# Another order of block products, the last units behind the last group, and joins and additions on GpSimd

## The reference

```
hm = rms_norm(x, g_pre_mlp[i])
f = jnp.square(jax.nn.relu(hm @ w_mlp_up[i])) @ w_mlp_down[i]
x = x + rms_norm(f, g_post_mlp[i])

gate = jax.nn.sigmoid(rms_norm(x, g_pre_ple[i]) @ w_ple_gate[i])
e = p[i] @ w_ple_proj[i]
x = x + rms_norm(gate * e, g_post_ple[i])
```

## Time and profile before

| | us |
|---|---|
| median of 3 runs | 2764.78 |
| the profiled execution | 2765.39 |
| its span | 2763.6 |
| TensorE busy | 2697.1 (98%) |
| VectorE busy | 2041.0 (74%) |
| ScalarE busy | 1395.6 (50%) |
| GpSimd busy | 291.1 (11%) |
| waits of TensorE's L1093 for DVE L2441, L2489 | 16.1 and 7.4 |

### The profile page before, as it was taken

One profiled execution on the slowest core, in us unless ns is written; L12 is line 12 of the kernel. 1 busy time (PEld: TensorE's weight loads), 2 busy tenths in 40 slices (PEclk: granted clock), 3 DMA queues, 4 the chain that ended last, 5 costly groups with the idle time before them and its releaser, 6 DMA issues.

```text
span 2763.6 us, 34607 instructions
## 1 busy us (share of the span) xinstructions
PE 2697.1 (98%) x12816; PEld 2242.8 (81%) x12816; DVE 2041.0 (74%) x2767; ACT 1395.6 (50%) x2399; POOL 291.1 (11%) x329
## 2 busy tenths in 40 slices
PE   8999999999999999989999999999999999999897
PEld 7878888888888888867888788888888888888685
DVE  5468888385777777788866688883767777777886
ACT  5337888464333333346644478884633333333473
POOL 0320000001111111100013200000010111111000
PEclk9999999999999999999999999999999999999998
DMA  4211112431111111132332111143311111112332
GB/s 163 78 57 48 33 34 95 157 111 65 62 54 54 54 39 57 58 136 85 106 113 76 51 40 34 29 146 120 137 39 48 60 62 51 51 38 67 123 106 76
DMA packets 86519, 208.28 MB, mean 75 GB/s; under 512 B 9040, under 2 KB 37840, under 8 KB 85328
## 3 DMA queue, kind: packets, MB, share of 16 engines
q1 hardware_dynamic: 86352, 206.07, 22.1%
HBM read 174.52 MB, written 31.52 MB: 75 GB/s over the span
## 4 chain that ended last, share of the span: by engine, by line
PE 90%; DVE 6%; ACT 1%; issue 1%; DMA 1%; POOL 0%; SPq 0%; DVEq 0%; ACTq 0%
PE ps L1093 27%; PE ps L1095 27%; PE ps L1094 27%; PE ps L1299 4%; PE ps L1324 2%; PE ps L1323 2%; DVE wl L2067 1%; DVE xf L2489 1%; DVE nm L2303 1%; DMA raw<-w_units 1%; DVE xf L2121 1%; PE ps L1132 0%; PE ps L1133 0%; DVE ptl L2310 0%; DVE xf L2124 0%
## 5 line engine op out<-in xcount | busy, mean ns | idle before, releaser
L1093 PE MATMUL ps<-hh,wh 128*128 128x512 f32 x2160 | 850.5, 394 | 15.6 <-DVE hl L2103 8.2
L1094 PE MATMUL ps<-hl,wh 128*128 128x512 f32 x2160 | 843.2, 390 | 0.0
L1095 PE MATMUL ps<-hh,wl 128*128 128x512 f32 x2160 | 843.0, 390 | 0.0
L1588 ACT ACTIVATE wh<-raw 128x256 fp32r<-128x256 f32 (+1 forms) x522 | 324.4, 639 | 429.9 <-PE ps L1095 273.3
L2067 DVE TENSOR_TENSOR wl<-raw,wh 128x256 fp32r<-128x256 f32 (+1 forms) x522 | 400.6, 787 | 142.3 <-ACT wh L1588 141.6
L1093 PEld LDWEIGHTS ps<-hh,wh 128*128 128x128 f32 x2160 | 407.4, 189 | 103.6 <-issue 11.6
L1094 PEld LDWEIGHTS ps<-hl,wh 128*128 128x128 f32 x2160 | 407.3, 189 | 87.1 <-issue 3.4
L1095 PEld LDWEIGHTS ps<-hh,wl 128*128 128x128 f32 x2160 | 407.1, 188 | 85.1
L2489 DVE TENSOR_TENSOR xf<-xf,ps 128x1024 f32<-128x1024 f32 x280 | 338.5, 1214 | 62.0 <-PE ps L1095 61.6
L1093 PE MATMUL ps<-hx,wh 128*128 128x512 f32 x448 | 174.3, 389 | 0.0
L1094 PE MATMUL ps<-hx,wh 128*128 128x512 f32 x448 | 174.3, 389 | 0.0
(11 more groups left out here) (233 smaller groups left out, 4252.0 us busy)
## 6 DMA issues: line engine op xcount, KB each, us to landing
raw<-w_units SPq DMA_DIRECT2D x182, 512.0 KB, 3.4
raw<-w_units SPq DMA_DIRECT2D x112, 256.0 KB, 2.9
x_mid<-xf SPq DMA_DIRECT2D x4, 2048.0 KB, 8.0
xf<-x_mid SPq DMA_DIRECT2D x4, 2048.0 KB, 8.3
hh<-mix_hi SPq DMA_DIRECT2D x14, 512.0 KB, 6.2
hl<-mix_lo SPq DMA_DIRECT2D x14, 512.0 KB, 7.2
stage<-w_head SPq DMA_DIRECT2D x16, 320.0 KB, 3.3
mix_hi<-cyh SPq DMA_DIRECT2D x8, 512.0 KB, 2.6
```

Of the source, the lines that this page charges most:

```text
L1093: nc.tensor.matmul(dst, ah, bh, start=start, stop=False)
L1094: nc.tensor.matmul(dst, ah, bl, start=False, stop=False)
L1095: return nc.tensor.matmul(dst, al, bh, start=False, stop=stop)
L1588: return nc.scalar.activation(dst, src, ACT.Copy, **more)
```

## The change

Four things change.

1. In all 14 groups (7 in each of 2 layers) the order of the turns is k = 1, 7, 5, 6, 2, 3, 4 instead of 1, 2, 3, 5, 6, 7, 4, GpSimd sums in the order (0,5), (1,5), (0,7), (1,7), (0,6), (1,6), (0,4), (1,4), and so for the second pair, and the uses and parts of `BIG_DVE` stand in another order. A product waits for its own hidden parts and no longer for the last.
2. In the last group the first seven parts stand directly behind `hidden.1.7`; all four last units come behind the 28 products on TensorE, so their loads come behind the quarters' on SP; `unit.4` stands behind `part.27`. Four PSUM pairs are used instead of three.
3. In the last group's lists stand two of the four joins (`whole.0`, `whole.1`) and some squares and their sums (`LAST_ACT`, `LAST_DVE`). The statistics matmul `post 1.0` stands behind the first of the last units instead of behind the last.
4. The other two joins and the eight additions to x of the first half (`add_x.1.0.c`, which on DVE ends after the multiplication) go to GpSimd. The lists of the rest of the MLP are in another order.

```diff
-TURNS = [(pair, k) for pair in (0, 2) for k in (1, 2, 3, 5, 6, 7, 4)]
+TURNS = [(pair, k) for pair in (0, 2) for k in (1, 7, 5, 6, 2, 3, 4)]
-HOME_BEFORE = [D_LAST[1], PLE_AT + 1]
+HOME_BEFORE = [D_LAST[0], PLE_AT + 1]
...
-    return (4, 6, 2, 0)[turn % 4] if G + 1 < BIG else (4, 6, 2)[turn % 3]
+    return (4, 6, 2, 0)[turn % 4]
...
 BIG_DVE = ...
-value.4.1 value.4.0 use.0 part.7 use.1 part.8 use.2 part.9 part.10 use.3 part.11 part.12 use.4 part.13 use.5
-part.14 use.6 part.15 part.16 use.7 part.17 use.8 part.18 use.9 part.19 part.20 use.10 part.21 use.11 part.22
-use.12 part.23 part.24 use.13 part.25 part.26 use.14 part.27 use.15 use.16 unit.5 use.17 use.18 use.19
+value.4.1 value.4.0
+use.0 part.7 use.1 part.8 use.2 part.9 use.3 part.10 use.4 part.11 use.5 part.12 use.6 part.13 part.14 use.7 part.15
+part.16 use.8 part.17 part.18 use.9 part.19 part.20 use.10 part.21 use.11 part.22 use.12 part.23 use.13 part.24 use.14
+part.25 use.15 part.26 use.16 part.27 use.17 unit.5 use.18 use.19
...
 MLP_DVE = steps("""
...
+sum_down.0.2 sum_down.0.3 sum_down.0.6 sum_down.0.7 value.30.0 low.98 rest.30.0 add_x.1.0.0 value.30.1
+add_x.1.0.1 rest.30.1 low.99 add_x.1.0.2 low.100 value.31.0 sum_chunk.1.0.1 add_x.1.0.3 rest.31.0 add_x.1.0.4
+sum_chunk.1.0.2 low.101 value.31.1 sum_chunk.1.0.3 add_x.1.0.5 rest.31.1 low.102 sum_chunk.1.0.4 add.31.0 add_x.1.0.6
...
 MLP_ACT = steps("""
...
+square_down.0.2 square_down.0.3 square_down.0.6 square_down.0.7 high.98 hidden.30.0 post.1.0 hidden.30.1 high.99
+chunk.1.0.0 high.100 chunk.1.0.1 hidden.31.0 high.101 chunk.1.0.2 hidden.31.1 high.102 chunk.1.0.3 chunk.1.0.4 high.103
...
+LAST_ACT = [(("part", 22), ("square_down", 0, 0)), (("part", 23), ("square_down", 0, 1)),
+            (("part", 24), ("square_down", 0, 4)), (("part", 25), ("square_down", 0, 5))]
+LAST_DVE = [(("use", 9), ("whole", 0)), (("part", 25), ("sum_down", 0, 1)), (("part", 26), ("sum_down", 0, 4)),
+            (("part", 27), ("sum_down", 0, 5)), (("use", 18), ("whole", 1))]
...
-    at = kept.index(("hidden", 1, 6)) + 1
...
+    at = kept.index(("hidden", 1, 7)) + 1
+    kept[at:at] = early
+    kept.remove(("unit", 4))
+    kept.insert(kept.index(("part", 27)) + 1, ("unit", 4))
...
-    ("up", 31, 1): [("post", 1, 0)],
+    ("up", 30, 0): [("post", 1, 0)],
...
-                    if n == 0:
-                        pe.wait_ge(big_lo, hidden_at(L, G, *HIDDEN_ORDER[-1]))
+                    if i == 0:
+                        pe.wait_ge(big_lo, max(hidden_at(L, G, c, o) for c in range(2) for o in (k, TURNS[0][1])))
...
-                        if g:
-                            pe.wait_ge(down_add, used_at(L, BIG - 1, len(TURNS) - 1))
+                        if i == 0:
+                            pe.wait_ge(down_add, used_at(L, BIG - 1, max(o for o in range(len(TURNS)) if banks_of(BIG - 1, o) == 2 * g)))
...
-                    else:
-                        last_units(0)
                     for n in range(MADE):
                         product(G, n)
+                last_units(0)
                 last_units(1)
...
+                if (k, t) == (1, 0):
+                    return
                 dve.wait_ge(post_mul, i)
                 V.tensor_tensor(xc, xc, f, ALU.add).then_inc(x_new, 1)
...
+                for m in (0, 2):
+                    pool.wait_ge(down_add, used_at(L, BIG - 1, TURNS.index((m, 4))))
+                    pool.wait_ge(down_whole, L * 4 + 2 + m // 2)
+                    f = facc[:, 1, m:m + 2, :]
+                    nc.gpsimd.tensor_tensor(f, f, facc[:, 1, m + QUARTERS:m + QUARTERS + 2, :], ALU.add).then_inc(down_whole, 1)
+                for c in range(DC):
+                    if c == 0:
+                        pool.wait_ge(x_home[0], L * 16 + 16)
+                    pool.wait_ge(post_mul, post_at(L, 1) * 16 + c + 1)
+                    nc.gpsimd.tensor_tensor(x[:, 0, c, :], x[:, 0, c, :], facc[:, 0, c, :], ALU.add).then_inc(x_new, 1)
```

More of the change, by code:

```diff
@@ L72 @@
 UP_LOADS = [[M_BIG if G + j == 0 else M_BIG + 8 * G + (j if j else -4) for j in range(4)] for G in range(BIG)]
-QUARTER_LOADS = [[M_BIG + 8 * G + (5 if G + 1 < BIG else 6) + i for i in range(QUARTERS)] for G in range(BIG)]
-U_LAST = (M_BIG + 8 * BIG - 4, M_BIG + 8 * BIG + 2)
+QUARTER_LOADS = [[M_BIG + 8 * G + (5 if G + 1 < BIG else 4) + i for i in range(QUARTERS)] for G in range(BIG)]
+U_LAST = (M_BIG + 8 * BIG, M_BIG + 8 * BIG + 2)
 D_LAST = (M_BIG + 8 * BIG + 4, M_BIG + 8 * BIG + 6)
@@ L270 @@
 sum.1.6 hidden.1.5 hidden.1.6 part.1 part.2 part.3 part.4 part.5 part.6 value.3.0 hidden.1.2 sum.1.3 hidden.1.3
-value.4.1 value.4.0 use.0 part.7 use.1 part.8 use.2 part.9 part.10 use.3 part.11 part.12 use.4 part.13 use.5
-part.14 use.6 part.15 part.16 use.7 part.17 use.8 part.18 use.9 part.19 part.20 use.10 part.21 use.11 part.22
-use.12 part.23 part.24 use.13 part.25 part.26 use.14 part.27 use.15 use.16 unit.5 use.17 use.18 use.19
+value.4.1 value.4.0
+use.0 part.7 use.1 part.8 use.2 part.9 use.3 part.10 use.4 part.11 use.5 part.12 use.6 part.13 part.14 use.7 part.15
+part.16 use.8 part.17 part.18 use.9 part.19 part.20 use.10 part.21 use.11 part.22 use.12 part.23 use.13 part.24 use.14
+part.25 use.15 part.26 use.16 part.27 use.17 unit.5 use.18 use.19
 """)
 MLP_ACT = steps("""
[L277 to L280, removed]
+square_down.0.2 square_down.0.3 square_down.0.6 square_down.0.7 high.98 hidden.30.0 post.1.0 hidden.30.1 high.99
+chunk.1.0.0 high.100 chunk.1.0.1 hidden.31.0 high.101 chunk.1.0.2 hidden.31.1 high.102 chunk.1.0.3 chunk.1.0.4 high.103
+chunk.1.0.5 square_down.1.0 chunk.1.0.6 square_down.1.1 chunk.1.0.7 high.104 high.105 high.106 square_down.1.2
 embed.0 square_down.1.3 embed.1 high.107 embed.2 pre.1.0 embed.3 high.108 embed.4 square_down.1.4 embed.5
@@ L293 @@
 MLP_DVE = steps("""
[L294 to L299, removed]
+sum_down.0.2 sum_down.0.3 sum_down.0.6 sum_down.0.7 value.30.0 low.98 rest.30.0 add_x.1.0.0 value.30.1
+add_x.1.0.1 rest.30.1 low.99 add_x.1.0.2 low.100 value.31.0 sum_chunk.1.0.1 add_x.1.0.3 rest.31.0 add_x.1.0.4
+sum_chunk.1.0.2 low.101 value.31.1 sum_chunk.1.0.3 add_x.1.0.5 rest.31.1 low.102 sum_chunk.1.0.4 add.31.0 add_x.1.0.6
+add.31.1 low.103 add.31.2 sum_chunk.1.0.5 add_x.1.0.7 chunk.1.0.0 chunk.1.0.1 sum_chunk.1.0.6 chunk.1.0.2 add.31.3
+sum_down.1.1 chunk.1.0.3 add.31.4 sum_chunk.1.0.7 chunk.1.0.4 add.31.5 low.104 chunk.1.0.5 low.105 chunk.1.0.6 low.106
+add.31.6 sum_down.1.2 chunk.1.0.7 add.31.7 sum_down.1.3
 low.107 low.108 sum_down.1.4 sum_down.1.5 sum_down.1.6 low.109 sum_down.1.7 low.110 z.0 add_x.1.1.0 low.111
@@ L323, in units_of @@
         return [UP_LOADS[G + 1][j - 4]]
-    return {4: [U_LAST[0]], 5: [U_LAST[1], U_LAST[1] + 1], 6: [U_LAST[0] + 1]}[j]
+    return [U_LAST[0] + j - 4]
+LAST_ACT = [(("part", 22), ("square_down", 0, 0)), (("part", 23), ("square_down", 0, 1)),
+            (("part", 24), ("square_down", 0, 4)), (("part", 25), ("square_down", 0, 5))]
+LAST_DVE = [(("use", 9), ("whole", 0)), (("part", 25), ("sum_down", 0, 1)), (("part", 26), ("sum_down", 0, 4)),
+            (("part", 27), ("sum_down", 0, 5)), (("use", 18), ("whole", 1))]
 def big_order(G, order):
@@ L332, in big_order @@
     kept = [e for e in order if e not in early and not (e[0] in ("square", "value") and e[1] == 4)]
-    at = kept.index(("hidden", 1, 6)) + 1
[L334 to L337, removed]
+    at = kept.index(("hidden", 1, 7)) + 1
+    kept[at:at] = early
+    kept.remove(("unit", 4))
+    kept.insert(kept.index(("part", 27)) + 1, ("unit", 4))
+    for before, step in LAST_ACT if order is BIG_ACT else LAST_DVE:
+        kept.insert(kept.index(before) + 1, step)
+    return kept
 def head_steps(h, order):
@@ L425 @@
         SQUARES += squares_of_in(layer, out)
-    for order in (MIX_ACT, mlp_order(layer, MLP_ACT)):
+    for order in (MIX_ACT, [step for _, step in LAST_ACT], mlp_order(layer, MLP_ACT)):
         SQUARES += squares_of(layer, order)
@@ L1442, in product @@
                         elif bank < 4:
-                            pe.wait_ge(up_v, up_at(L, G, 3, 0) if bank else up_at(L, G + 1, 0, 0))
+                            pe.wait_ge(up_v, up_at(L, G, 3, 0) if bank else up_at(L, G + 1, 0, 0) if G + 1 < BIG else up_at(L, G, 2, 0))
                         elif G:
@@ L1983, in down_square @@
                     else:
[L1984 removed]
+                        act.wait_ge(down_out, down_at(L, BIG - 1, PRODUCTS.index((QUARTERS - 1, 1))))
                         if m < QUARTERS:
[L1986 removed]
+                            act.wait_ge(down_add, used_at(L, BIG - 1, TURNS.index((m // 2 * 2, 2))))
                         else:
@@ L2052, in big_steps @@
                             big_unit(G, *n)
+                        elif kind == "square_down":
+                            down_square(*n)
                 big_square(0, 0, 1)
@@ L2493, in whole @@
                     t, m = n // 2, 2 * (n % 2)
-                    dve.wait_ge(down_add, used_at(L, BIG - 1, len(TURNS) - 1))
```

(5 more changed lines are left out.)

12 lines of the change are left out of this document (5 added, 7 removed).

## The result

The changed kernel takes 2790.93 us, median of 4 runs (2786.25 to 2791.66), and the kernel before 2765.22 beside it (4 runs, 2764.25 to 2767.42). The ratio is 1.0086, interval 1.0070 to 1.0102: 25.7 us slower, in the direction and inside the range of the forecast (2784, 2750 to 2796), 0.9 us above what the prediction calls the forecast's own range (2776 to 2790). The profiled execution took 2791.66 us with a span of 2789.8, against 2763.6 before: 26.2 us to place.

What follows compares the result with a forecast made beforehand. DVE's list, with loads and ACT between, was taken to set the MLP's end, where 20.4 us a layer are lost; 2765.4 + 3.6 (group ends) + 15 (both layers' ends) = 2784 us, range 2750 to 2796.

Steps and rivals of the forecast that it cites:

- product 7 waits: Last group: DVE gives a use and part each 1.47 us, TensorE eats a product in 1.36; wait up to 1.4.
- product 14 waits: Last group: part 14 is split only at 21.3 to 22.75 us, so this product waits 1.7 us.
- second halves: Down products needing rest.31.1 and low.102: low.102 ends at 91.2 us, TensorE idle 8 us, then clock fall 2.4.
- The last group: Up to the last units: use.0 starts at 7.9 to 9.3, not 2.92; products end at 42.3 to 44.3, not 38.1.
- GpSimd blocks DVE: MLP end: DVE's two-SBUF-operand instructions wait for GpSimd's; joins cost 3.7 us, five additions 5.3; end 12 us a layer later.
- The rival with hidden work: MLP end: DVE loses nothing to GpSimd, 3.9 to 6.3 us less a layer, 2756 us; chance 0.28.
- The detour over ACT: Rest of MLP: sum_chunk.3 before rest.31.1 waits for ACT's chunk 3, 3.3 us in DVE's list.
- From the second unit to low.102: DVE's list from 68.3: 12 instructions 12.9 us, blocked additions 5.3, ACT detour 3.3; low.102 ends at 91.2.
- The stretch in sum: From last group's products to `embed`: +6.9 to +8.3 us a layer, 7.5 taken, +15 in both.
- the group ends: 12 places where the next group's second unit is ready at 37.9 to 38.6, wanted 38.1; 0.3 each, +3.6 us.
- Much slower: the groups lose too: Rival: each of 12 group ends waits 1.0 us and the MLP end costs 8.3 a layer; 2794 us, chance 0.17.
- Clock: Behind the idle before first last unit, second unit and second halves, TensorE's clock falls, about 2.4 us each.

Runs made afterwards that it cites:

- x_both_dve: Changed kernel with the two joins and eight additions to x of each layer back on DVE: 2772.88 us, ratio 1.0021 to the kernel before.
- b_pool: Kernel before with joins whole.2 and whole.3 and the eight additions to x moved to GpSimd, orders left alone: 2773.38 us, ratio 1.0018.
- x_detour: Changed kernel with the third sum of squares (sum_chunk.1.0.3) moved behind low.102 in DVE's list: 2779.98 us, ratio 1.0047 to the kernel before.
- b_turns: Kernel before with only the new order of turns, GpSimd's sums, and uses and parts in DVE's group list: 2782.27 us, ratio 1.0051.
- b_turns_list: Kernel before with the new order of turns, sums, uses and parts, but parts 24 to 27 earlier in DVE's list: 2764.82 us, ratio 0.9991.
- combo3: Changed kernel, joins/additions on DVE, parts 24-27 earlier, sum_chunk.1.0.3 behind low.102; last group: unit.4 behind use.17, parts 2-6 behind hidden.1.6: 2749.83 us, ratio 0.9932.
- combo1: Changed kernel with joins and additions on DVE, parts 24-27 earlier, sum_chunk.1.0.3 behind low.102, last group's unit.4 behind use.17: 2752.53 us, ratio 0.9945.

## Why the prediction was right

By its own steps, layer 0 in the count of the forecast:

| step | forecast | measured |
|---|---|---|
| use.0 | 7.9 to 9.3 | 8.6 |
| product 7 waits | up to 1.4 | 0.5 |
| product 14 waits | 1.7 (+0.5 in others) | 1.4, the next 0.8 |
| end of products | 42.3 to 44.3 | 44.0 |
| first last unit | 45.7 to 47.8, idle 3.5 | 47.3, idle 3.25 |
| statistics | 57.3 to 59.2, idle 3.6 | 58.6, idle 4.08 |
| value of the second unit | 68.3 | 68.2 |
| second halves | 91.2, idle 8 | 90.1, idle 6.99 |
| `embed` | 110.3 to 111.7 | 110.4 |

- **The last group.** Taking away the 10.88 us of units between the up units and the products delayed use.0 by as much as the chain of value, hidden and parts said, and the products ended in the forecast's bounds. Only in the size of single waits was it off: product 7 waited a third of what was allowed.
- **GpSimd blocks DVE.** The one overlapping pair of the earlier trace rows decided the sign, and it held. The joins cost sum_down 3.3 us (6.39 less 3.08), forecast 3.7. The two joins took 5.15 us beside the sums where I took 2 x 2.37. DVE's two-operand instructions over 1 us beside additions came as named. By the rule of the Trainium skill (SBUF — State Buffer, "Who interferes with whom") an instruction with a single SBUF input is free; the value at 1240.96 agrees with its 0.68 us. The test on the kernel as a whole is x_both_dve (-18.0) and b_pool (+5.7). The rival with hidden work (2756) falls with them. The forecast shared the blocking out as 3.7 us for the joins and 5.3 for the additions; by the runs on the changed kernel nearly all of the gain comes with the joins (stretch 11.0 us shorter in both layers, with the additions as well 12.5), since additions that block 4.4 us a layer also spare DVE 3.1.
- **The detour over ACT.** Forecast 3.3 us of wait in DVE's list, measured 3.29; with what followed, x_detour's 11.0 us in both layers.
- **From the second unit to low.102.** The forecast's terms were 12.9, 5.3 and 3.3 us behind 68.3, which add up to 89.8; the text wrote 91.2. low.102 ended at 89.9: the blocked instructions cost 4.4 and not 5.3, the rest of the list 14.1 and not 12.9. That the end came within 1.3 us of the text is luck in part, since these errors have opposite signs.
- **The stretch in sum.** 7.0 and 7.1 us a layer, where 7.5 was taken.
- **The step that was mis-sized: the group ends.** The forecast put 0.3 us on each of 12, 3.6 in all, with 1.0 as the bound. The ends lose 0.3 to 1.5 us each; from start to start layer 0 loses 4.5 and layer 1 5.4, so 9.9, near 0.8 each. In the other kernels with the same lists it was 6.5 to 8.8, in b_turns some 11: never near 3.6. The estimate of 37.9 to 38.6 for the unit against 38.1 wanted was made from single typical rows and its middle taken (its terms give 37.8 and 38.5). TensorE only loses by lateness and never gains by earliness, so the mean of the losses lies above the loss at the mean; that this is the whole reason is an argument and not tested. With 9.9 for 3.6 the forecast would have been 2790, the measured 2790.9. So the measured time lies nearer to the rival "Much slower: the groups lose too" (2794, with 1.0 us at each end, chance 0.17) than to the forecast (2784, with 0.3, chance 0.45), and that rival told the group ends better. b_turns_list says that it was the list and not the order. The forecast saw that "the second half of DVE's list is full", but took the list as part of the order.
- **Clock.** A fall was forecast behind all three waits. It came each time. Behind the first last unit's wait in layer 0 (3.25 us idle) the next starts are 0.30 and 0.34 us apart and then eight of 0.43 or a little less, 1.7 us in all; in layer 1, behind 3.81, 1.4 us. The granted clock in layer 0 (stretch, then PE, PEld, DVE, ACT, POOL, clock, DMA, GB/s):

```profile
1214.90:1217.50 2.60, 2.60 (x7) 2.00 (x7) 2.57 (x3) 0.31 (x1) 0.00 (x0) 0.50 0.57 191
```

The forecast took 2.4 for each. In layer 0 the fall behind this wait is nearly free, as the statistics behind this unit wait anyway: in x_detour's layer 0 no fall came behind 3.29 us, and the statistics waited 5.69 instead of 4.08.

Open: the parts alone on the kernel before sum to 20.3 us (14.6 and 5.7) of the 25.7. The other 5 belong to what is left, the moved last units with their lists, the fourth PSUM pair and the other place of x's return; no run took any of that alone. And of the 26.2 us of span, 24.0 are placed (14.1 and 9.9). Of the rest, 1.8 us lie between layer 0's `embed` and the first products of layer 1. That distance is 783.1 us before and 784.9 after; in b_pool, with the orders of the kernel before, it is 786.5, and over all kernels it goes from 783.1 to 786.5, so the 1.8 can be scatter.

## What to carry to other kernels

An elementwise instruction with two SBUF operands moved from DVE to GpSimd need not be taken off DVE: 20 of them moved left DVE's busy time as it was or 4.3 us higher. Where DVE has such an instruction next, count what is left of GpSimd's own, up to nearly its whole length (0.68 became 2.58). Move it only where DVE is idle or reads PSUM. When the order of the bottleneck's work changes, write the feeding engine's list anew: the small steps that start a load for the next round go ahead of the bulky ones that nobody waits for. A margin of zero costs something in every round; charge it with the lateness of the slower rows, not with the difference of typical ones.

## What the runs showed that was not expected

- The blocking costs both sides: GpSimd's 128x512 addition took 1.27 us with DVE idle and 1.64 to 2.21 beside DVE's. A 128x1024 addition of two SBUF operands took about 2.6 (5.15 and 5.21 for two) beside DVE's sums; what it takes alone no run shows.
- The idle time alone did not tell whether the clock falls. It fell behind 3.25 us (changed kernel), 2.15 (combo3) and 1.85 (x_both_dve's statistics, one start of 0.81 and then seven of 0.43), and it did not behind 3.29 and 3.23 (x_detour) or 2.46 (combo1). A forecast should give such a fall a chance and not a certainty.
- Behind a wait the statistics' matmuls stretch with the clock like the others. In layer 1 of the changed kernel:

```profile
2593.90 0.77 PE L1101 MATMUL ps<-hh,wh 128*128 128x512 f32 x1 [3.81 <-DVE xf L2500]
2594.46 0.63 PE L1102 MATMUL ps<-hl,wh 128*128 128x512 f32 x1
...
2604.79 2.07 PE L1168 MATMUL ps<-accy,ones_r 128*128 128x512 f32 x2 [3.85 <-DVE accy L2106]
2605.88 1.42 PE L1101 MATMUL ps<-hh,wh 128*128 128x512 f32 x1
2607.09 0.63 PE L1102 MATMUL ps<-hl,wh 128*128 128x512 f32 x1
```

The two statistics matmuls and the one behind them take from 2604.79 to 2607.09, 2.30 us. In combo1, where the wait was 1.92 us and no fall came, they take 1.19 (1216.14 to 1217.33). That is 1.1 us more, but it is part of the fall and does not come on top: to the last slow start the fall costs 2.9 and 2.7 us at the statistics of the two layers, and 2.6 and 2.5 behind the waits of 6.99.
